# A decoder layer on one core: the first attention's logits from per-head keys, 64 deep, two heads side by side in the row halves of the array

## The reference, cut to what matters

```python
q = q.reshape(B, S, N_HEADS, HEAD_DIM)                 # 8 heads of 64
q_lat = jnp.einsum('bshd,chd->bshc', q, w_uk[l])       # queries absorbed into the latent space, 128 deep
c = rms_norm(c, kv_norm_g[l])
...
logits = jnp.einsum('bqhc,bqkc->bqhk', qb, c_sel).astype(jnp.float32) * HEAD_DIM ** -0.5
...
logits = jnp.where(valid[:, :, None, :], logits + bias, -jnp.inf)
p = jax.nn.softmax(logits, axis=-1).astype(c_sel.dtype)
return jnp.einsum('bqhk,bqkc->bqhc', p, c_sel)
```

## Time and profile before

| | |
|---|---|
| median of 3 runs | 1243.11 us (1242.24 to 1243.94) |
| the profiled execution | 1247.31 us, span 1245.5 us |
| PE busy | 1194.9 us, 96% of the span |
| DVE, ACT, POOL busy | 848.2, 546.4, 522.8 us (68, 44, 42%) |
| chain that ended last | PE 79%, POOL 8%, DVE 6%, issue 3% |
| granted PE clock, mean | 0.988 of full speed |

### The profile page before, as it was taken

The page is one execution under the profiler, slowest core; times in us unless marked ns, Lnnn a source line. Parts: engine busy times, 40 slices in busy tenths (PEclk is TensorE's granted clock), DMA queues, the critical chain, the costliest instruction groups (busy, mean ns, idle before and its releaser), DMA issues.

```text
span 1245.5 us, 16284 instructions
## 1 busy us (share of the span) xinstructions
PE 1194.9 (96%) x5551; PEld 962.0 (77%) x5551; DVE 848.2 (68%) x1275; ACT 546.4 (44%) x891; POOL 522.8 (42%) x420
## 2 busy tenths in 40 slices
PE   5999999889999999999999999989899999999997
PEld 4776687668788778778788778978788888888886
DVE  6388987777857888888988878858433333333357
ACT  4545543765165244244244276651342443433440
POOL 2235794855345676776775653221002102003002
PEclk9999899989999999999999999999999999999999
DMA  7733432011314333233243200044223323332331
GB/s 224 253 77 95 159 85 68 1 42 63 100 35 135 99 104 118 85 120 100 86 133 101 89 14 1 1 153 119 85 86 101 105 98 93 110 101 85 118 102 68
DMA packets 126853, 118.63 MB, mean 95 GB/s; under 512 B 5773, under 2 KB 99530, under 8 KB 126794
## 3 DMA queue, kind: packets, MB, share of 16 engines
q1 hardware_dynamic: 126794, 117.86, 31.0%
HBM read 107.34 MB, written 10.50 MB: 95 GB/s over the span
## 4 chain that ended last, share of the span: by engine, by line
PE 79%; POOL 8%; DVE 6%; issue 3%; ACT 2%; DMA 2%; POOLq 0%; DVEq 0%; SPq 0%; ACTq 0%
PE g_bank L1679 15%; PE g_bank L1680 15%; PE g_bank L1681 15%; PE wide L1679 8%; PE wide L1681 8%; PE wide L1680 8%; PE g_bank L1841 3%; POOL wlo L458 3%; PE g_bank L1639 2%; POOL rows L872 2%; PE wide L1799 1%; PE wide L1743 1%; PE wide L1744 1%; POOL rstd L784 1%; DMA wring<-in_w_up 1%
## 5 line engine op out<-in xcount | busy, mean ns | idle before, releaser
L458 POOL TENSOR_TENSOR wlo<-wring,whi 128x1024 fp32r<-128x1024 f32 (+1 forms) x94 | 230.0, 2448 | 206.3 <-ACT whi L1546 123.3
L1679 PE MATMUL g_bank<-xhi,whi 128*128 128x512 f32 (+2 forms) x768 | 302.2, 394 | 4.8 <-DVE xlo L699 3.9
L1681 PE MATMUL g_bank<-xhi,wlo 128*128 128x512 f32 (+2 forms) x768 | 298.8, 389 | 0.0
L1680 PE MATMUL g_bank<-xlo,whi 128*128 128x512 f32 (+2 forms) x768 | 298.8, 389 | 0.0
L1546 ACT ACTIVATE whi<-wring 128x1024 fp32r<-128x1024 f32 x120 | 127.1, 1059 | 355.9 <-PE wide L1681 179.8
L458 DVE TENSOR_TENSOR wlo<-wring,whi 128x1024 fp32r<-128x1024 f32 (+1 forms) x66 | 84.4, 1279 | 197.8 <-ACT whi L1546 192.7
L1679 PE MATMUL wide<-whi,hhi 128*128 128x512 f32 x480 | 190.2, 396 | 0.7 <-POOL wlo L458 0.7
L1680 PE MATMUL wide<-wlo,hhi 128*128 128x512 f32 x480 | 189.6, 395 | 0.0
L1681 PE MATMUL wide<-whi,hlo 128*128 128x512 f32 x480 | 189.6, 395 | 0.0
L1679 PEld LDWEIGHTS g_bank<-xhi,whi 128*128 128x128 f32 (+1 forms) x768 | 145.6, 190 | 40.5 <-issue 4.4
L1681 PEld LDWEIGHTS g_bank<-xhi,wlo 128*128 128x128 f32 (+1 forms) x768 | 145.5, 190 | 33.1 <-issue 0.9
(11 more groups left out here) (244 smaller groups left out, 1939.6 us busy)
## 6 DMA issues: line engine op xcount, KB each, us to landing
wring<-in_w_up SPq DMA_DIRECT2D x64, 512.0 KB, 4.1
wring<-in_w_down SPq DMA_DIRECT2D x64, 512.0 KB, 3.7
wring<-in_w_in SPq DMA_DIRECT2D x26, 512.0 KB, 3.9
wring<-in_w_o SPq DMA_DIRECT2D x16, 512.0 KB, 4.5
rows<-in_x SPq DMA_DIRECT2D x8, 512.0 KB, 4.9
normalized_rows<-rows SPq DMA_DIRECT2D x8, 512.0 KB, 6.9
rows<-normalized_rows SPq DMA_DIRECT2D x4, 512.0 KB, 5.1
emb_stage<-normalized_rows SPq DMA_DIRECT2D x4, 512.0 KB, 4.6
```

The source lines that it names most:

```text
L458: eng.tensor_tensor(parts_of(name, lo_tile(name)), parts_of(name, wring[n % 4]), parts_of(name, hi_tile(name)).bitcast(F32), ALU.subtract) ...
L1679: nc.tensor.matmul(out_ap, w_hi, m_hi, start=first, stop=False)
L1680: nc.tensor.matmul(out_ap, w_hi, m_lo, start=False, stop=False)
L1681: return nc.tensor.matmul(out_ap, w_lo, m_hi, start=False, stop=last)
```

## The change: what it does

- `latent_queries(0)` goes. In its place `keys()` makes four matmuls of 128 rows, each the keys of two heads (`wuk_again`, the raw w_uk loaded once more, against `latT`), which ScalarE copies out, scaled, to `kT0`. Heads 2p and 2p + 1 lie in the two halves of its rows.
- The queries of the first chunk are kept: GpSimd copies `qT` to `qT0` in four pieces (`keep_queries`), two ahead of each of two splits, once 16 scores are added. ScalarE waits for `q_kept` before it writes `qT` for the second chunk.
- SyncE waits for the normalized latents and loads `wuk_again` between two weight units.
- ScalarE no longer waits for `score_added` 16 before its copies.
- The first attention's logits come in batches of two heads, same block (`early_logits`): steps m and m + 2, 64 rows deep, one from the upper and one from the lower half, into the two 512-column banks of `wide[m % 2]` (`wide_of`). They are issued at steps 3 and 0 (mod 4), one step ahead, instead of two steps ahead in every step. DVE's waits for them count accordingly.
- The second attention is as it was. ScalarE's copies for the folds and the early values also stay as they are.

```diff
     names = ["vecs"] + [("xT", 0, k) for k in range(KT)] + chunk_uses(0)
-    names += [("near", n) for n in range(4)] + [("ql", 0, h) for h in range(HEADS)]
+    names += [("near", n) for n in range(4)] + [("kk", 0, p) for p in range(4)]
     names += [("xT", 1, k) for k in range(KT)] + chunk_uses(1)
...
         mask = part("mask", 24, [P, 2, S])
-        qlatT = part("qlatT", 32, [P, HEADS, CHUNK])
+        kT0 = part("kT0", 32, [P, 4, CHUNK])
+        qT0 = part("qT0", 40, [P, 4, CHUNK])
+        wuk_again = part("wuk_again", 76.25, [P, HEADS * HD])
         qlat_hi = part("qlat_hi", 32, [P, HEADS, CHUNK], F32R)
...
             return rec_wide0[:, w % 2, :] if w < 8 else qT[:, 1, w % 2 * 2 * P:w % 2 * 2 * P + 2 * P]
+
+        def wide_of(m):
+            return wide[m % 2][:, m % 4 // 2 * 512:m % 4 // 2 * 512 + 512] if m < 32 else wide[m % 2][:, :]
...
         logits_full = sem("logits_full")
+        q_kept = sem("q_kept")
         masked = sem("masked")
...
                          ).then_inc(bias_in, 16)
-            load_units(units[7:U[("iq", 1, 3)]])
+            load_units(units[7:9])
+            sp.wait_ge(lat_ready, CB)
+            sp.dma_start(wuk_again[:, :], w_uk.rearrange("o c h d -> (o c) (h d)")).then_inc(late_in, 16)
+            load_units(units[9:U[("iq", 1, 3)]])
             for b in range(CB):
...
             x_lo(pool, "xT", 1, x_lo_pool)
-            lo(("iq", 1, 0), ("iq", 1, 1))
+
+            def keep_queries(pieces):
+                pool.wait_ge(score_added, 16)
+                pool.wait_ge(g_evac, EV[("q", 0, 3)])
+                for k in pieces:
+                    pool.tensor_copy(qT0[:, k, :], qT[:, k, :]).then_inc(q_kept, 1)
+
+            keep_queries((0, 1))
+            lo(("iq", 1, 0))
+            keep_queries((2, 3))
+            lo(("iq", 1, 1))
...
                 length = (i + 1) * P
-                dve.wait_ge(logits_full, m + 1)
+                dve.wait_ge(logits_full, m + 1 if m >= 32 else m - m % 4 + 2 + m % 2 * 2)
                 dve.wait_ge(mask_full, m + 1)
                 if m >= 2:
                     i2 = block_head(m - 2)[0]
                     dve.wait_ge(g_full, EV[("tr", m - 2, (i2 + 4) // 4 - 1)])
-                nc.vector.tensor_tensor_reduce(logit[:, m % 2, 0:length], wide[m % 2][:, 0:length],
+                nc.vector.tensor_tensor_reduce(logit[:, m % 2, 0:length], wide_of(m)[:, 0:length],
                                                mask[:, m % 2, 0:length], -1.0, -TAKEN, ALU.add, ALU.min,
...
                     if name[0] == "q":
+                        if c:
+                            act.wait_ge(q_kept, 4)
                         copy_out(name, qT[:, n, :], bank(name)[:, :])
...
-            def latent_queries(c, heads=range(HEADS)):
-                for h in heads:
-                    copy_out(("ql", c, h), (qlat_hi if c else qlatT)[:, h, :], bank(("ql", c, h))[:, :], scale=HD ** -0.5)
+            def latent_queries():
+                for h in range(HEADS):
+                    copy_out(("ql", 1, h), qlat_hi[:, h, :], bank(("ql", 1, h))[:, :], scale=HD ** -0.5)
+
+            def keys():
+                for p in range(4):
+                    copy_out(("kk", 0, p), kT0[:, p, :], bank(("kk", 0, p))[:, :], scale=HD ** -0.5)
...
                          bank(("near", n))[:, :].rearrange("p (h n) -> p h n", h=2))
-
-            act.wait_ge(score_added, 16)
-            latent_queries(0)
+            keys()
             transposed(1, "xT", emb_g, emb_b, x_lo_pool, 0)
...
             mlp_groups(0)
-            latent_queries(1)
+            latent_queries()
...
-            def latent_queries(c, heads=range(HEADS)):
-
-                evacuated(("q", c, 3))
-                for h in heads:
-                    name = ("ql", c, h)
+            def keys():
+
+                evacuated(("cT", 0))
+                pe.wait_ge(late_in, 16 * 6)
+                for p in range(4):
+                    name = ("kk", 0, p)
+                    free(name)
+                    nc.tensor.matmul(bank(name)[:, :], wuk_again[:, p * P:p * P + P], latT[:, 0:CHUNK],
+                                     start=True, stop=True).then_inc(g_full, 1)
+
+            def latent_queries():
+
+                evacuated(("q", 1, 3))
+                for h in range(HEADS):
+                    name = ("ql", 1, h)
                     free(name)
...
+            def early_logits(m):
+
+                for n in (m, m + 2):
+                    i, h = block_head(n)
+                    half = slice(h % 2 * HD, h % 2 * HD + HD)
+                    if n >= 4:
+
+                        pe.wait_ge(masked, n - 3)
+                    nc.tensor.matmul(wide_of(n)[:, 0:(i + 1) * P], qT0[half, h // 2, i * P:i * P + P],
+                                     kT0[half, h // 2, 0:(i + 1) * P], start=True, stop=True).then_inc(logits_full, 1)
+
             def logits(m):
                 i, h = block_head(m)
-                if m >= 32:
-                    pe.wait_ge(qlat_lo_ready, h + 1)
+                pe.wait_ge(qlat_lo_ready, h + 1)
                 length = (i + 1) * P
-                if m >= 2:
+                if m >= 34:
                     pe.wait_ge(masked, m - 1)
                 at = slice(i % CB * P, i % CB * P + P)
                 for k0 in range(0, length, 512):
-                    k1 = min(length, k0 + 512)
-                    if i < CB:
-                        last = nc.tensor.matmul(wide[m % 2][:, k0:k1], qlatT[:, h, at], latT[:, k0:k1], start=True, stop=True)
-                    else:
-                        k1 = max(k1, k0 + 256)
-                        last = three_passes(wide[m % 2][:, k0:k1], qlat_hi[:, h, at], qlat_lo[:, h, at],
-                                            latT_hi[:, k0:k1], latT_lo[:, k0:k1], True, True)
+                    k1 = max(min(length, k0 + 512), k0 + 256)
+                    last = three_passes(wide[m % 2][:, k0:k1], qlat_hi[:, h, at], qlat_lo[:, h, at],
+                                        latT_hi[:, k0:k1], latT_lo[:, k0:k1], True, True)
                 last.then_inc(logits_full, 1)
             def attention(c):
                 lo, hi = 32 * c, 32 * c + 32
                 if c == 0:
-                    evacuated(("ql", c, 7))
+                    evacuated(("kk", 0, 3))
+                    pe.wait_ge(q_kept, 4)
                     pe.wait_ge(relu_ready, 16)
                 else:
                     pe.wait_ge(relu_ready, 48)
                     pe.wait_ge(latT_lo_ready, 2)
-                logits(lo)
-                logits(lo + 1)
+                for m in (lo, lo + 1):
+                    if c:
+                        logits(m)
+                    else:
+                        early_logits(m)
                 for k in range(2, NB) if c else ():
                     values(1, k)
                 for step in range(lo, lo + LAST_STEP):
-                    if step + 2 < hi:
+                    if c and step + 2 < hi:
                         logits(step + 2)
+                    if c == 0 and step % 4 in (0, 3) and 0 < step < hi - 1:
+                        early_logits(step + 1)
                     for name in attention_step(c, step):
...
                                  start=True, stop=True).then_inc(g_full, 1)
-            latent_queries(0)
+            keys()
             x_transposes(1, "xT")
             keys_queries(1)
             products(1)
             attention(0)
             output_projection(0)
             mlp_groups(0)
-            latent_queries(1)
+            latent_queries()
             attention(1)
```

## The result

The changed kernel takes 1254.95 us (four executions, 1253.4 to 1256.99) against 1243.53 for the kernel before on the same chip: ratio 1.0099, interval 1.0081 to 1.0116, **11.4 us slower**. 1243.3 was forecast, with 1247 as the upper end: wrong side and outside the range.

What follows compares the result with a forecast made beforehand. TensorE (PE), busiest and 79% of the last chain, was taken as the bound. Stretch before -0.8, first half +0.2, second half +0.8: +0.2 us, moved to the median 1243.3 us; 8-in-10 range 1239 to 1247 us.

Steps and rivals of the forecast that it cites:

- The keys: Stretch before the first attention: four full matmuls replace eight half-row ones, -1.0 us; -0.8 taken because of the clock.
- The pairing: First attention's logits on PE: two heads in different row halves run side by side, a pair at one head's price plus 0.4 us.
- The mechanism of the second half: Steps 16 to 31: DVE idles for the odd batch, and nothing of PE's relief comes through.
- Term of the second half: Steps 16 to 31 of the first attention: +0.1 us for each of three periods, +0.5 in the last, +0.8 together.
- T + 3.7: Second half: when DVE sees the odd block's batch, counted from T, where PE goes on to logits after the reciprocals' transposes.
- T + 7.3: Second half: end of one four-step period counted from its start T, against 7.16 us in the kernel before.
- the chain stretches: Rival, slower: a value product waits for a fold, second-half periods get 1 us longer, 1246.3 us; chance 0.14.
- Term of the first half: Steps 0 to 15: period T + 4.5 against 4.54 us, so zero, with +0.2 for the group between the halves.
- the lower clock: Inside the attention, where PE has more idle time: listed among signs that would prove the forecast wrong; no size or chance.
- 4.2 below it: Whole kernel: median of runs, 1243.11 us, lies 4.2 below the profiled execution's 1247.31; used to move the forecast to the median.
- changes of rows hidden: Rival, faster: the 0.2 us row changes in the attention fall under waits for ScalarE or DVE, 1238.8 us; chance 0.23.
- no pairing: Rival, slower: a batch's heads run one after the other on PE, +8.6 us, 1252 us; chance 0.05.

Runs made afterwards that it cites:

- filled gaps: Changed kernel with unused identity products put into PE's waits in steps 0 to 3 of the first attention (8, 4, 4, 4): 1250.42 us, ratio 1.0060.
- the second profile: The changed kernel, unedited, timed and profiled once more beside the kernel before: 1254.19 us, ratio 1.0090.
- the pairs two steps ahead: Changed kernel with both heads' 64-row logits issued two steps ahead, at steps 2 and 3 (mod 4): 1243.79 us, ratio 1.0032.
- the order alone: Kernel before with the changed kernel's batches of two at steps 3 and 0 (mod 4), logits still 128 rows deep: 1255.81 us, ratio 1.0095.
- the cheap exchange: Kernel before with odd steps' value products issued behind that step's transposes, first attention only: 1240.36 us, ratio 0.9972. In both attentions: 1268.46 us, ratio 1.0205.

## Why the prediction was wrong, step by step

**Right.** The keys: -1.05 us at the transposes of x where -1.0 was summed. By the first mask it is -1.6 in the two traces, but this stretch varies by itself: it is 106.4 to 107.6 us in the six traces with latent queries and 105.6 to 106.3 in the ten with keys and no fall at 189 us, 1.1 apart in the mean, where -0.8 was summed. The pairing, with gaps of 0.09 us where rows change (four transposes from 258.05, at 0.11 us each, end at 258.49; the logits start at 258.58). GpSimd's copies and SyncE's transfer are hidden: the splits behind the copies still wait for ScalarE, 2.47 and 2.08 us, and the weights land by 61 us. The mechanism of the second half: DVE idle for the odd batch, nothing of PE's relief coming through.

**Term of the second half, mis-sized.** "T + 3.7" for the odd mask was 4.22 from the start of the batch (255.56 to 259.78), "T + 7.3" was 7.87, "+0.8 us" was 29.6 - 27.0 = 2.6. The step that failed is the value product put straight behind the batch: it waits 0.53 us for a fold that DVE makes late because of the last odd mask. With the product behind the transposes PE waits for no fold and no low parts in this half, and the period is 7.4, close to the sum's 7.3. That is the rival "the chain stretches", priced at 1 us a period and measured at 0.7, and given 0.14. I had its condition (each product's bank waits for the fold four uses back) and did not walk DVE's list once round the period to see whether it was met.

**Term of the first half, wrong.** "Zero, with +0.2" was +3.9. The sum followed one chain at full clock. It named the lower clock as what would make it wrong, but gave it no price and no chance. At least 1.8 us are the clock (filled gaps); the rest, at most 2.2, I put down to the wait for odd batches, which is still 1.22 us at 234.30 with the clock back. The earlier trace rows had PE idle for 3.5 us of that half; the change took the logits and the early values out of where PE had least else to do. In the four microseconds behind the first mask 2.83 us of work became 1.22, and the 1.2 GHz level came inside of them, or 1.4 us behind them in the second profile. The Trainium skill (TensorE: Matmul & The Clock Gate, What's actually happening) says that activity is what releases the throttle; the traces agree: products of the identity put into those steps kept the clock at 1.00. I had no term for it in the sum.

**The step from the profiled execution to the median, wrong.** "4.2 below it" is not a constant of the kernel. It is that this execution had 30 us at the lower clock and the usual one 15. The changed kernel has 0.980 to 0.985 in all nine timed executions, 38 to 50 us, mostly 40. By these figures 25 us more at 0.4, an estimate, is 10 us, of which the attention's own fall is part.

The 11.4 us, with the pieces measured: -1.1 to -1.6 for the keys, +2.6 in the second half, at most +2.2 for the order in the first half, together 3.2 to 3.7; about 8 are left for the clock. The one execution of the changed kernel with a filled start that had a clock of 0.994 took 1246.18 us, 2.9 above what the kernel before takes on average at that clock (1243.3). Filling the start gives back 3.8 of the 8 in the medians, at least 1.8 of them inside the attention.

**What stays open:** the other 4 us. The trace shows where such a piece lies. Both profiled kernels have two more falls behind the attention (at 270.7 and 342.3 before, at 277.4 and 349.1 after, 10.2 us together), where the code of both is the same. In the six traces that have both of them the time from the last mask to the end is 981.6 to 982.2 us; in eight that have neither, and no products put in at the end, it is 976.2 to 978.0. Since both have them, the two traces are only 7.4 us apart. Most executions of before can't have them: their clock of 0.994 or more is 15 us of the lower level or less, and the trace of the pairs two steps ahead, which has neither fall, already holds 17.7 us of it in other places. All nine of the changed kernel have 0.985 or less, room for both. Only one execution in each set has a trace, so where the clock falls in the others isn't known, and why falls outside the attention come more often with this change is not shown. Work at the attention's end was no cure.

The other rivals: *changes of rows hidden* is refuted by the gaps, *no pairing* by the pairs. That the order and not the rows is the loss is shown from both sides: the order alone, with full rows, has the ratio 1.0095, and the paired rows gain 3 to 5 us over full rows in equal order, which only makes up for the 4 us that the batches two steps ahead cost with full rows.

## What to carry to other kernels

Before a batch is made earlier, look at what it was doing where it stood: here work that waited filled TensorE's gaps, and where it was gone the clock fell. In lists taken in order, walk each engine's list once round the period with the new times, and count every "waits for the one four back" as a term, not as a rival. Compare executions at equal mean granted clock, and ask of a profile first whether its clock is the usual one. And the cheap exchange beside the large change was the better one: look at what stands ahead of the wait that the chain shows, in each stage by itself, for in the second attention the same exchange makes the stage 22 us longer. And an engine recorded as busy throughout need not be what sets the pace.

## What the runs showed of the hardware that was not expected

- One and the same kernel, the one two steps ahead, takes 1241.6 or 1253.8 us by its mean granted clock (0.994 or 0.983): 0.4 us for each us at the lower level, in kernels whose PE is busy 95% of the time.
- With single heads in half the rows PE was recorded busy for 30.00 of 30 us at a granted clock of 0.50, in a fall of 61 us; with pairs the clock was 1.00 at 22.91 of 28.10.
- The fall at 222.8 us came with no idle time of PE longer than 0.76 us in the 7 us ahead of it: the work was thin, 0.72 us in the last two.
- Some 27 small products put into waits of PE cost 2.8 us of masks, though each was put where PE waits for an exponential.
- The same half of an attention, with PE recorded full in both orders, took 27.0 and 24.9 us.
